# Input projection of a hybrid encoder block: one level of Strassen's scheme for the query, key and mLSTM q/k columns, tokens in two rounds

## The reference, cut to what matters

```python
u = _rmsnorm(h, pre_norm_w[i])                 # 2048 tokens x 1024
proj = u @ w_in[i]                             # 1024 x 4616 columns
sb_q, sb_k, sb_v, sb_z, ml_q, ml_k, ml_v, ml_o, ml_z, ml_i, ml_f = _split_cols(proj)
y_sb = _stick_breaking_attention(...) ; ...    # needs q, k, v of all heads
qk = silu(_causal_conv(concat([ml_q, ml_k]), ml_conv_w[i], ml_conv_b[i]))
y_ml = _mlstm_chunkwise(...) ; y = concat([y_sb, y_ml]) @ w_out[i] ; ...
```

## Time and profile before

| | |
|---|---|
| median of three runs | 1812.4 us |
| span of the profiled execution (1808.6 us), below the median by | 3.8 us |
| PE busy | 1761.9 us, 97% |
| DVE, ACT, POOL busy | 1119.1, 991.3, 680.6 us |
| input projection up to the last gate matmul | 0 to 487.3 us |
| matmuls of the four groups | 116.6 to 472.3 us |
| first matmul of the attention | 494.94 us |

### The profile page before, as it was taken

The page is one execution under the profiler, slowest core; times in us unless marked ns, Lnnn a source line. Parts: engine busy times, 40 slices in busy tenths (PEclk is TensorE's granted clock), DMA queues, the critical chain, the costliest instruction groups (busy, mean ns, idle before and its releaser), DMA issues. The chain is left out here.

```text
span 1808.6 us, 28177 instructions
## 1 busy us (share of the span) xinstructions
PE 1761.9 (97%) x8972; PEld 1437.3 (79%) x8972; DVE 1119.1 (62%) x1776; ACT 991.3 (55%) x2041; POOL 680.6 (38%) x942
## 2 busy tenths in 40 slices
PE   7999999999899999999999999998999999999998
PEld 6888888878577887888878887886788888788887
DVE  5431214555479898979797979894666666533333
ACT  5431213322277787878787878784677776411111
POOL 1100000000147777777777777772234444200000
PEclk9999999999999999999999999999999999999999
DMA  6677766121394647454656453735555454422220
GB/s 199 163 192 215 232 186 186 52 87 47 126 282 131 172 144 212 135 175 135 174 171 185 135 176 127 249 118 190 169 193 159 162 189 139 162 77 79 81 82 40
DMA packets 193733, 277.05 MB, mean 153 GB/s; under 512 B 66684, under 2 KB 128380, under 8 KB 184408
## 3 DMA queue, kind: packets, MB, share of 16 engines
q1 hardware_dynamic: 190952, 265.19, 47.8%
q0 software_dynamic: 2672, 10.52, 1.7%
HBM read 187.41 MB, written 88.26 MB: 152 GB/s over the span
## 5 line engine op out<-in xcount | busy, mean ns | idle before, releaser
L975 PE MATMUL b_late<-w_split,spare 128*128 128x512 f32 x1416 | 411.4, 415 | 2.5 <-ACT b_p_out L1057 2.3
L756 POOL TENSOR_TENSOR b_a_lo<-b_aT,b_a_hi 128x512 fp32r<-128x512 f32 (+2 forms) x312 | 354.8, 1137 | 25.0
L1138 DVE TENSOR_TENSOR_SCAN b_buf<-b_y,b_buf 128x511 f32<-128x511 f32 (+2 forms) x320 | 357.9, 1118 | 9.1
L529 PE MATMUL a_po<-uT_hi,w_split 128*128 128x512 f32 x1024 | 318.6, 392 | 2.3 <-DVE w_split L397 2.3
L975 PEld LDWEIGHTS b_late<-w_split,spare 128*128 128x128 f32 x1416 | 243.4, 190 | 40.5 <-issue 4.6
L752 POOL CAST b_a_hi<-b_aT 128x512 fp32r<-128x512 f32 (+1 forms) x320 | 182.1, 569 | 179.1 <-PE b_o L949 147.6
L1148 DVE SCALAR_TENSOR_TENSOR b_buf<-b_buf,b_y 128x512 f32<-128x512 f32 (+2 forms) x320 | 187.9, 587 | 70.0 <-PE b_y L935 69.0
L529 PEld LDWEIGHTS a_po<-uT_hi,w_split 128*128 128x128 f32 x1024 | 193.0, 188 | 46.4 <-DVE w_split L397 2.7
L1034 ACT ACTIVATE b_aT<-b_turned 128x512 f32<-128x512 f32 (+1 forms) x320 | 170.3, 532 | 67.6 <-POOL b_a_lo L756 60.1
L529 PE MATMUL a_po<-uT_lo,w_split 128*128 128x512 f32 x512 | 201.6, 394 | 0.0
L1043 ACT ACTIVATE b_buf<-b_y 128x512 f32<-128x512 f32 (+2 forms) x320 | 171.3, 535 | 50.1 <-PE b_y L929 47.7
(11 more groups left out here) (244 smaller groups left out, 3359.6 us busy)
## 6 DMA issues: line engine op xcount, KB each, us to landing
spare<-u_pair SPq DMA_DIRECT2D x62, 1024.0 KB, 5.4
proj_n<-b_p_out SPq DMA_DIRECT2D x59, 256.0 KB, 5.7
c_gates<-proj_n SPq DMA_DIRECT2D x16, 768.0 KB, 4.5
w_raw<-in_w_in POOLq DMA_DIRECT2D x5, 2048.0 KB, 10.1
x_in<-in_x SPq DMA_DIRECT2D x16, 512.0 KB, 3.9
qk_hi<-stage_hi SPq DMA_DIRECT2D x32, 256.0 KB, 2.6
qk_lo<-stage_lo SPq DMA_DIRECT2D x32, 256.0 KB, 2.9
u_pair<-uT_hi SPq DMA_DIRECT2D x16, 512.0 KB, 3.7
```

The source lines that it names most:

```text
L529: mm = pe.matmul(po[t][:], w[:, k, m * P:(m + 1) * P], u[:, k, t * GROUP:(t + 1) * GROUP], start=(k == 0 and n == 0), stop=(k == KT - 1 an ...
L756: nc.gpsimd.tensor_tensor(lo[:, cols], raw, hi[:, cols].bitcast(F32), ALU.subtract).then_inc(lo_done, 1)
L975: mm = pe.matmul(late[:], u_in[f % US][:, u_part, k, :], w[:, k, :], start=(i == 0), stop=(i == PASSES - 1))
L1138: nc.vector.tensor_tensor_scan(down, y[u % YS][:, 1:keys][:, ::-1], down, b[:, keys - 1:keys], ALU.add, ALU.subtract).then_inc(log_done, 1)
```

## The change

The columns of q, k, ml_q and ml_k are made in chunks of 256 columns by 1024 tokens. A chunk is a 2 x 2 product of half matrices (k in halves of 512, columns in halves of 128, tokens in halves of 512). Seven half products of 12 matmuls (4 k x 3 parts) replace eight: 84 matmuls for 96. Operands: `A11`, `A12`, `A22` and four sums `S1` to `S4` of the weights; `B11`, `B21`, `B22` and four differences `T1` to `T4` of the activations. Results pile up in three PSUM banks (`X`, `Y`, `Z`, two sets), and `combine` reads a bank between two products of it.

Since `u` now takes seven half tiles, hi and lo, tokens go in two rounds (`PAIRS`) of eight tiles: in each round eight v tiles, then eight chunks. Weights of v are loaded and split twice, those of the chunks are loaded twice (1 MB each, from SP's queue). POOL now makes the weight sums, their low parts, `T3`, `T4`, the low parts of `T` and of three results out of four. `scale` works in place (`x_in` for `xn`), so the next load of x waits until the tile is transposed. All loops of the stage are written out. The attention and everything after are the same, but for one more wait, on the last stores of `ml_t`.

```diff
-            def load_x(q, j):
-                i = j % 2
-                sp.wait_ge(x_read, 4 * q + (j + 1))
+            def load_x(s):
+                if s >= 2 and s % TILES_OF_PAIR >= 2:
+                    sp.wait_ge(xpose_done, 2 * (s - 1))
...
+            def load_chunk(n):
+                    sp.wait_ge(plain_lo_done, 3 * n)
+                    sp.wait_ge(sums_made, 4 * n)
+                    sp.wait_ge(sums_lo_done, 4 * n - 1)
+                sp.dma_start(chunk_raw, w_view[:, :, column(n):column(n) + CHUNK]).then_inc(chunk_loaded, 16)
...
+                # SP, a v tile of a round
+                    if r + 2 < TILES_OF_PAIR:
+                        load_x(s + 2)
+                    if r % 2 == 1:
+                        store_b12(s)
+                    if r > 0:
+                        store_v(s - 1)
...
+                # ACT, a v tile: s odd / even
+                        high(s)
+                        if r % 2 == 0:
+                            keep_raw(s)
+                        else:
+                            differences_hi(s)
+                    if r + 2 < TILES_OF_PAIR:
+                        square(s + 2)
+                    if r > 0:
+                        v_high(s - 1)
...
+                # POOL, a v tile
+                    if r % 2 == 1:
+                        third(s)
+                        difference_lo(s, 0)
+                        fourth(s)
+                        difference_lo(s, 1)
+                    if r + 2 < TILES_OF_PAIR:
+                        root(s + 2)
+                    if r % 2 == 1:
+                        difference_lo(s, 2)
+                        difference_lo(s, 3)
...
+                # POOL, a chunk (qk: results to be split; m: results to be convolved)
+                        make_sum(n + 1, "S1")
+                        make_sum(n + 1, "S3")
+                        sum_lo(n + 1, "S1")
+                        make_sum(n + 1, "S2")
+                        c_low(n, "c22")
+                        sum_lo(n + 1, "S2")
+                        make_sum(n + 1, "S4")
+                        sum_lo(n + 1, "S3")
+                        c_low(n, "c12")
+                        sum_lo(n + 1, "S4")
+                        c_low(n, "c21")
...
+                # DVE, a chunk
+                    if after_conv:
+                        taps(n - 1, 1, (0, 1))
+                    second(n)
+                    if after_conv:
+                        taps(n - 1, 1, (2, 3))
+                    if more:
+                        plain_lo(n + 1, "A11")
+                    third_and_c22(n)
+                    if kind_of(n) == "qk":
+                        c11_low(n)
+                    if more:
+                        plain_lo(n + 1, "A12")
+                    c12(n)
+                    if kind_of(n) == "m":
+                        taps(n, 0, (0, 1))
+                    c21(n)
+                    if kind_of(n) == "m":
+                        taps(n, 0, (2, 3))
+                    if more:
+                        plain_lo(n + 1, "A22")
...
+            def product(n, slot):        # PE; slots A11, S2, S1, S3, A12, S4, A22
+                for k in range(HALF):
+                    for i, (w_part, u_part) in enumerate(PARTS):
+                        mm = pe.matmul(banks[bank, set_of(n)][:], (op_hi, op_lo)[w_part][a][:, k, :],
+                                       (u_hi, u_lo)[u_part][b][:, k, :], start=(slot < 3 and k == 0 and i == 0),
+                                       stop=(k == HALF - 1 and i == 2), skip_group_check=(slot >= 3))
+                mm.then_inc(product_done, 1)
```

More of the change, by code:

```diff
@@ L144, in input_projection @@
[L144 to L167, removed]
@@ new lines, in set_of, with factor, place, token_tile @@
+        def set_of(n):
+            return (n + n // CHUNKS) % 2
+        def factor(n):
+            kind, i = CHUNK_ORDER[n]
+            return -SB_SCALE if kind == "qk" and i < 2 else 1.0
+        def place(s):
+            j, r = s // TILES_OF_PAIR, s % TILES_OF_PAIR
+            return j, r // 2, r % 2
+        def token_tile(s):
+            j, i, side = place(s)
+            return TILES_OF_PAIR * j + i + HALF * side
+        def couple(s):
+            return s // 2
+        def v_bank(s):
+            j, i, side = place(s)
+            return banks["XY"[side], 1 - j]
@@ new lines, in low @@
+            def low(s):
+                j, i, side = place(s)
+                cols = slice(i * P, (i + 1) * P)
+                for h in range(2):
+                    if h == 0 and side == 1:
+                        hi, target = b12_hi[:], b12_lo[:]
+                    else:
+                        q = ("B11", "B21", "B22")[h + side]
+                        hi, target = u_hi[q][:, :, cols], u_lo[q][:, :, cols]
+                    dve.wait_ge(u_hi_done, 2 * s + h + 1)
+                    nc.vector.tensor_tensor(target, pt[h][:].rearrange("p (k t) -> p k t", k=HALF), hi.bitcast(F32),
+                                            ALU.subtract).then_inc(u_lo_done, 1)
@@ L474, in _ @@
+            taps(SUBS - 1, 1, range(CONV_K))
+            read_gates(1)
         @block.tensor
@@ L476, in _, with turn @@
             PARTS = ((1, 0), (0, 1), (0, 0))
-            def turn(q, j):
-                i = j % 2
-                pe.wait_ge(x_read, 4 * q + (j + 3))
+            def turn(s):
+                pe.wait_ge(scaled, s + 1)
+                until(pe, u_lo_done, 2 * s)
+                if s > 0 and s % 2 == 1:
+                    pe.wait_ge(a_raw_done, 2 * couple(s - 1) + 2)
+                if s > 0 and s % 2 == 0:
+                    pe.wait_ge(t12_done, 2 * couple(s - 1) + 2)
+                if s == TILES_OF_PAIR:
+                    for t in range(2):
+                        pe.wait_ge(gates_read[t], 1)
@@ L536, in _ @@
[L536 to L547 removed]
+                        if k < HALF:
+                            u = ((b12_hi, b12_lo)[u_part][:, k, :] if side else (u_hi, u_lo)[u_part]["B11"][:, k, cols])
+                        else:
+                            u = (u_hi, u_lo)[u_part][("B21", "B22")[side]][:, k - HALF, cols]
@@ new lines, in _ @@
+            pe.wait_ge(ident_ready, 1)
+            for j in range(PAIRS):
+                s0, n0 = TILES_OF_PAIR * j, CHUNKS * j
+                for r in range(TILES_OF_PAIR):
+                    s = s0 + r
+                    if s == 1:
+                        times_v(0, range(HALF))
+                    if s != TILES_OF_PAIR:
+                        turn(s)
+                    if r > 0:
+                        times_v(s - 1, range(HALF, KT) if s == 1 else range(KT))
+                times_v(s0 + TILES_OF_PAIR - 1)
+                for c in range(CHUNKS):
+                    if c == CHUNKS - 2 and j == 0:
+                        gate_columns(0)
+                    for slot in range(len(SLOTS)):
+                        if c == CHUNKS - 1 and j == 0 and slot == len(SLOTS) - 1:
+                            turn(TILES_OF_PAIR)
+                        product(n0 + c, slot)
```

1092 lines of the change are left out of this document (750 added, 342 removed).

## The result

The changed kernel takes 1918.3 us (1916.8 to 1919.3) beside 1812.4 for the one before: 1.0586 times as long (95% interval 1.0571 to 1.0601), 106 us more. The forecast was +56 and a range up to 1908: the sign held, the size didn't.

A forecast was written before the change was run, and what follows sets the result against it. PE, busy 97%, was taken to bound the kernel before, chains of other engines the changed one. -43.9 + 27 + 38 + 31 + 3.5 = +55.6 on 1808.6 gives 1864.2, forecast 1868 us; range 1820 to 1908.

The forecast's parts named there:

- What goes: Stage's matmuls: 1344 in chunks for 1536, at 0.232 us each 311.8 us against 355.7, so -43.9 us.
- The v stretch: v tiles: a circle without PE takes 20.2 us for two tiles; +27 us in round 1, +38 in round 2.
- The chunks: Sixteen chunks: circles of 22.7 us (m) and 22.0 (qk) over PE's 19.5, together +31 us.
- The load: Chunk weights: 1 MB lands in 5.4 us, felt by twelve of sixteen chunks; -18 or +56 us at the ends.
- rival 3: POOL beside DVE: its operations take 1.70 us for 1.29, +42 us, 1910 in all; chance 0.12.
- Neither holds from the first chunk: Chunks at a round's ends: first ones are prepared before, the last prepares nothing, so 0 to 1 us over in most.
- The end: End of the stage: PE idles about 11 us for 7.61 behind C21, six taps, a silu and stores; +3.5 us.
- PE's slow clock within the slack: v stretch: PE's idling brings the low clock, about eight matmuls at 0.427, 1.6 us more a tile, hidden in the slack.

The follow-up runs named there:

- e2: Changed kernel with S1's product issued twice in each chunk (192 more matmuls, same result): 1918.5 us.
- f2: Changed kernel with another order in the v stretch alone (v's parts ahead of next square and scale, x loaded before v is stored): 1891.0 us.
- e1: Changed kernel without the product of low weights by high activations in the chunks, 448 of 1344 matmuls: 1915.9 us.
- e4: Changed kernel with POOL's four low parts of the sums made for one quarter of their columns, from a round's second chunk on: 1888.1 us.
- e3: Changed kernel loading only half of a chunk's weights (512 KB for 1 MB) from a round's second chunk on, the rest stale: 1892.0 us.
- h1: Changed kernel with DVE's three low parts of a chunk made for one quarter of their columns, from a round's second chunk on: 1906.1 us.
- f1: Changed kernel with another order at the ends of rounds alone (second half of v's or output's weights split behind C21 and taps): 1893.9 us.
- g2: f4 with A22's low part and load moved earlier, activation stores later, and a second P1 buffer in chunks 5, 9 and 11: 1841.8 us.
- g3: g2 with only the first tap of m chunks' first half between C12 and C21, the other three behind A22's low part: 1848.1 us.
- f3: Changed kernel with chunk weights loaded in three parts, A11, A21 and A12 ahead of a chunk's last stores, A22 at the old place: 1903.0 us.
- f4: Changed kernel with the edits of f1, f2 and f3 together, and the v stretch's new order also at the start of round 2: 1857.7 us.

## Why the prediction was wrong

- *What goes, -43.9.* Right as a count, priced 7 us too low: PE took 0.227 a matmul in the chunks and not 0.232. e2 shows that the changed kernel doesn't feel it.
- *The v stretch.* Right by place: PE waited for `a_pt`'s inputs, and f2 shows the circle. The size is right in part by luck. A couple took 20.4 us for 20.2, but the couple's second scale took 2.28 beside a POOL operation where I had 1.28 (six of the sixteen scales did), and the 1.0 that I had added for hand-overs covered it. In round 2 the wait at the start was 15.7 us and not 9, since the low part of the second tile stands behind the scale of the third; and only six tiles were held by the circle and not eight, since the first two had been transposed during chunk 7 and right behind it. The two errors cancel. (A load of x stands behind the stores of the v tile four before, and not three, as the text on the change has it; the circle is the same.)
- *The chunks, +31.* This is the step that failed, by size: +76. The mechanism, a circle of load, POOL and DVE with PE outside, held (e1 to e4). (a) The load: I took 5.4 from the row of the same size and wrote "with 1 KB runs it may be more"; it was 6.4. From e3, 1.9 us of load are worth 26, so 1.0 is some 14 by estimate. (b) DVE and POOL on each other: I priced DVE's low part at 0.69 and the first tap at 1.09 (2 x 0.547) from rows where POOL stood still, and gave the slow row to rival 3 as POOL's alone. It is DVE that stretched most: +1.05 (A12's low part), +0.8 (first tap) and +0.4 (halo) in one m circle, and POOL 0.3 to 0.45 in two or three operations. Over the whole stage DVE's records are 42 us longer than the same operations alone, POOL's 20; not all of that lies in a circle. h1 and e4 show that it is real; their -12 and -30 contain narrower work too, so its own share isn't separated. (c) "Neither holds from the first chunk": the first chunks of both rounds took 24 us, the second of round 2 23.3, and chunk 7 26.5, where DVE has the scale of the next round's tile, which waits for a load, ahead of C22. I had them at 20.5 and 19.6. This is 17 of the 45 us.
- *The end, +3.5.* Failed: +12.9. I counted C21 and six taps but not the low parts of weights ahead of them, which wait for their load. With those moved behind the taps (f1) PE's idle time was 11.6, where I had 11.
- *PE's slow clock within the slack.* Right in the changed kernel (e1, e2); for g2 and g3 it is open.
- *Rivals.* Rival 3's time, 1910, was the nearest, but it had half of the effect: POOL's S3 rose to 1.55 on average, and DVE's low part, which it left alone, went from 0.69 to 1.22.

## What to carry to other kernels

When work is moved from the bound engine to engines with strict lists, sum up the longest circle, not the loads, and take for each operation the duration that it has beside its new neighbour, which can be its own and the whole of the neighbour's instruction. In each list look at what stands ahead of the operation that ends the stage: here it was a wait for an unrelated load. Where one circle is opened, another may stand close behind it (P1's store: at most 3 us alone, 23 after).

## What the runs showed of the hardware

- A DVE low part, halo copy, scale or tap, which reads SBUF alone, waited for the end of a POOL tensor_tensor that was running when it started: its record ended a fixed time after POOL's (low part of 512 columns 0.55, of 128 columns 0.15, halo copy 0.03, scale 1.08), and was longer by up to one POOL operation (3 columns: 0.16 to 1.27; 512: 0.68 to 1.74). POOL waited for DVE in the same way (1.29 became 1.6 beside a low part, 2.15 beside a tap of 1024 columns). DVE combinations with one input in PSUM took 0.68 or 0.69 throughout.
- 1 MB of weights from SP's queue in runs of 1 KB landed in 6.4 us, 512 KB in 4.5 (e3); the 256 KB of A22 took 3.8 to 6.5 in f3. A store issued 2 us behind loads of 768 KB took 5.2 us for 3.2 (f4).
